# Attention probabilities and values as half precision pairs in a one-core trunk kernel

## The reference

```python
def _attend_block(qn, qr, qpos, kn, kr, v, kpos):
    s = jnp.einsum('bqhd,bkhd->bhqk', qn, kn) + jnp.einsum('bqhd,bkd->bhqk', qr, kr)
    s = s.astype(jnp.float32) * ATTN_SCALE
    allowed = (kpos // CHUNK)[None, :] <= (qpos // CHUNK)[:, None]
    s = jnp.where(allowed[None, None], s, -jnp.inf)
    p = jax.nn.softmax(s, axis=-1)
    return jnp.einsum('bhqk,bkhd->bqhd', p.astype(v.dtype), v)
```

## Time and profile before

| what | value |
|---|---|
| median of 3 runs | 1024.31 us (1024.24 to 1025.77) |
| the profiled execution's own time | 1023.69 us |
| its span in the profile | 1021.8 us |
| TensorE matmul busy | 980.3 us, 96% |
| TensorE weight loads busy | 759.5 us, 74% |
| VectorE busy | 814.5 us, 80% |
| ScalarE busy | 655.9 us, 64% |
| bytes moved | 205.01 MB, mean 201 GB/s |

### The profile page before, as it was taken

How to read it: one execution, slowest core, us unless ns; L and a number is a source line. 1 busy time by engine, 2 the same in 40 slices (tenths; PEclk the granted TensorE clock), 3 DMA queues, 4 the chain that set the end, 5 groups by cost and what they waited for, 6 DMA issues and landing times.

```text
span 1021.8 us, 24221 instructions
## 1 busy us (share of the span) xinstructions
PE 980.3 (96%) x9926; PEld 759.5 (74%) x9926; DVE 814.5 (80%) x1470; ACT 655.9 (64%) x1057; POOL 0.7 (0%) x10
## 2 busy tenths in 40 slices
PE   8999999999999999999999999999999989999995
PEld 6877777777776799976568777777777768998653
DVE  4897777654689899998888877776448899999986
ACT  5675454754355799876767645556543659987864
POOL 0000000000000000000000000000000000000000
PEclk9999999999999999999999999999999999999998
DMA  9845544423465199998736544452334435999961
GB/s 347 307 167 164 149 140 127 135 84 104 144 229 165 59 331 360 358 366 312 281 126 215 173 125 141 139 151 91 104 119 151 145 102 164 358 366 364 371 237 54
DMA packets 59651, 205.01 MB, mean 201 GB/s; under 512 B 7216, under 2 KB 10348, under 8 KB 59020
## 3 DMA queue, kind: packets, MB, share of 16 engines
q1 hardware_dynamic: 55980, 195.95, 55.2%
q10 hardware_dynamic: 3552, 7.42, 2.0%
HBM read 198.76 MB, written 3.40 MB: 198 GB/s over the span
## 4 chain that ended last, share of the span: by engine, by line
PE 64%; DVE 22%; DVEq 6%; ACT 4%; issue 3%; SPq 1%; DMA 1%; ACTq 0%
PE bank L1786 37%; DVE wlo L1075 12%; PE bank L1810 4%; DVEq L1709 4%; PE bank L2324 3%; ACT whi L556 2%; PE bank L2156 2%; PE bank L1815 1%; PE bank L2011 1%; DVE xT L1088 1%; DVE mo L1711 1%; DVE xlo L1094 1%; PE bank L2045 1%; DVE acc L1084 1%; PE bank L2087 1%
## 5 line engine op out<-in xcount | busy, mean ns | idle before, releaser
L1075 DVE SCALAR_TENSOR_TENSOR wlo<-w,whi 128x1024 f16<-128x1024 f32 x358 | 428.9, 1220 | 61.5 <-ACT whi L556 59.5
L556 ACT ACTIVATE whi<-w 128x1024 f16<-128x1024 f32 x358 | 369.0, 1049 | 81.4 <-PE bank L1786 48.1
L1786 PE MATMUL bank<-xhi,whi 128*128 128x320 f16 x688 | 206.2, 300 | 1.1 <-DVE wlo L1075 1.1
L1786 PE MATMUL bank<-xhi,wlo 128*128 128x320 f16 x688 | 205.7, 299 | 0.0
L1786 PE MATMUL bank<-xlo,whi 128*128 128x320 f16 x688 | 205.7, 299 | 0.0
L1786 PE MATMUL bank<-arena_b,whi 128*128 128x112 f16 x2048 | 161.7, 213 | 7.8 <-DVE wlo L1075 6.7
L1786 PEld LDWEIGHTS bank<-arena_b,whi 128*128 128x128 f16 x2048 | 149.5, 98 | 12.9 <-issue 9.0
L1786 PE MATMUL bank<-arena_b,wlo 128*128 128x112 f16 x1024 | 157.3, 213 | 0.0
L1786 PEld LDWEIGHTS bank<-arena_b,wlo 128*128 128x128 f16 x1024 | 100.1, 98 | 0.0
L1786 PEld LDWEIGHTS bank<-xhi,whi 128*128 128x128 f16 x688 | 67.2, 98 | 31.2 <-issue 3.0
L1786 PEld LDWEIGHTS bank<-xhi,wlo 128*128 128x128 f16 x688 | 67.3, 98 | 26.2
(11 more groups left out here) (379 smaller groups left out, 1761.1 us busy)
## 6 DMA issues: line engine op xcount, KB each, us to landing
w<-in_w SPq DMA_DIRECT2D x358, 512.0 KB, 5.1
arena_b<-head_rows ACTq DMA_DIRECT2D x2, 1920.0 KB, 7.1
xT<-in_x SPq DMA_DIRECT2D x2, 640.0 KB, 5.6
out_y<-xT SPq DMA_DIRECT2D x4, 320.0 KB
rows<-in_rows ACTq DMA_DIRECT2D x1, 1024.0 KB, 10.7
rows<-in_rows SPq DMA_DIRECT2D x1, 1024.0 KB, 6.4
out_ckv<-arena_a SPq DMA_DIRECT2D x2, 320.0 KB
acc<-kr SPq DMA_DIRECT2D x2, 288.0 KB
```

The source lines that it names most:

```text
L556: A(whi[:, n % SLOTS, :], w32[:, n % RAW, :], ACT.Copy, scale=WS).then_inc(hi_done.sem, 1)
L1075: V.scalar_tensor_tensor(wlo[:, n % SLOTS, :], w32[:, n % RAW, :], WS, whi[:, n % SLOTS, :], ALU.mult, ALU.subtract).then_inc(lo_done.sem, 1)
L1786: ins = M(out, w[:, s, sub * P:(sub + 1) * P], rhs(part, k), start=(n == 0), stop=(n == 3 * len(subs) - 1))
```

## The change

Probabilities and values are held as half precision pairs. A value item is copied by ScalarE in half precision (`v_out_hi`) and VectorE subtracts it for the rest (`v_out_lo`). The exponentials go to a single f32 buffer; VectorE multiplies the reciprocal by 4096; ScalarE writes the scaled probabilities in half precision (`probs_hi`) and VectorE the rest (`probs_lo`). The transposes are two matmuls each with a half precision identity, summed in PSUM; the result is split again by `columns_hi` and `columns_lo`. The values are three half precision products each. Turns are reordered: on TensorE the filler comes ahead of the values of u - 2 and the transposes of u - 1; on the other two engines the columns of u - 2 open the turn and the split of u closes it; rotation and query copies of half 1 move into turn 1, the rotation's sum into turn 2 ahead of the wait for the exponentials.

```diff
 # ScalarE
+                def probs_hi(u):
+                    act.wait_ge(p_inv.sem, p_inv.value(l, u + 1))
...
                 q_out(0)
                 hi_a(0)
                 k_out(0)
                 hi_a(1)
+                v_out_hi(0)
                 hi_a(2)
                 for u in range(UNITS):
+                    if u == 3:
+                        k_out(1)
+                    if u >= 2:
+                        columns_hi(u - 2)
                     if u in (5, 8, 11):
                         out_hi(u // 3 - 1)
-                    if u == 2:
-                        q_out(1)
-                    elif u == 3:
-                        k_out(1)
-                    elif u != 4:
+                    if u == 4:
+                        v_out_hi(1)
+                    elif u not in (2, 3):
                         gate_tanh(FILLER[u - 1] if u else 2)
-                    if u:
-                        probs_out(u - 1)
                     exps(u)
                     if u != 3:
                         hi_a(FILLER[u])
+                    if u == 1:
+                        q_out(1)
+                    probs_hi(u)
 # VectorE
                 for u in range(UNITS):
+                    if u >= 2:
+                        columns_lo(u - 2)
                     if u in (5, 8, 11):
                         out_lo(u // 3 - 1)
-                    if u == 2:
-                        rotate(1)
                     if u == 4:
-                        v_out(1)
+                        v_out_lo(1)
...
                     V.tensor_scalar(sm[:, 2:2 + w], sm[:, 0:w], -ATT_SCALE, None, ALU.mult
                                     ).then_inc(s_max.sem, 1)
+                    if u == 1:
+                        rotate(1)
+                    if u == 2:
+                        rotated(1)
                     dve.wait_ge(p_exp.sem, p_exp.value(l, u + 1))
                     V.reciprocal(sm[:, 6:6 + w], sm[:, 4:4 + w])
                     dve.drain()
...
+                    V.tensor_scalar(sm[:, 6:6 + w], sm[:, 6:6 + w], PS, None, ALU.mult
+                                    ).then_inc(p_inv.sem, 1)
-                    if u == 2:
-                        rotated(1)
                     if u != 3:
                         lo_a(FILLER[u])
+                    probs_lo(u)
 # TensorE
+                    def weigh(out, kt, rows_, vc, at, first, last):
+                        for x, y in ((0, 0), (0, 1), (1, 0)):
+                            a = M(out, v_hl[0:rows_, hf, x, kt, vc], prob_t[0:rows_, u % 2, y, at],
+                                  start=(first and x == 0 and y == 0), stop=(last and x == 1))
+                        return a
...
                 for u in range(UNITS):
                     scores(u)
-                    if u:
-                        transposes(u - 1)
-                    if u >= 2:
-                        values(u - 2)
...
                         gate(FILLER[u])
+                    if u >= 2:
+                        values(u - 2)
+                    if u:
+                        transposes(u - 1)
```

More of the change, by code:

```diff
@@ L64 @@
 GS = 1024.0
+PS = 4096.0
 BRANCHES = (1, 2, 0)
@@ L323, in build_trunk @@
         q_rot = sig("q_rot", 2)
+        v_hi = sig("v_hi", 6)
         v_ev = sig("v_ev", 6)
@@ L537, in _ @@
             nc.gpsimd.memset(gm16[:, :, :], 0.0).then_inc(consts_set.sem, 1)
-            for first in (num_ps, att_done, dc_ps, h_done, g_done, s_ps, sp_ps, o_lo, t_sb, stored, c_stored,
+            for first in (num_ps, att_done, dc_ps, h_done, g_done, s_ps, sp_ps, o_lo, t_lo, stored, c_stored,
                           m_used, yg_lo, e_free, e_prod, ot_ev):
@@ L782, in k_out, with v_out_hi @@
                         a.then_inc(qk_ev.sem, 1)
+                def v_out_hi(hf):
+                    if hf:
+                        act.wait_ge(stored.sem, stored.value(l, 16 * 4))
+                    for n in range(3):
+                        act.wait_ge(*item_done(l, hf, 8 + n))
+                        b = item_bank(ITEM0[hf] + 8 + n)
+                        if n < 2:
+                            a = A(v_hl[:, hf, 0, 2 * n:2 * n + 2, :], b[:, :].rearrange(
+                                "p (i n) -> p i n", i=2), ACT.Copy, scale=UN * XS)
+                        else:
+                            a = A(v_hl[0:TS, hf, 0, 4, :], b[0:TS, 0:2 * P], ACT.Copy, scale=UN * XS)
+                        a.then_inc(v_hi.sem, 1)
                 def gate_tanh(a):
@@ L2056, in transposes @@
                 def transposes(u):
-                    pe.wait_ge(p_norm.sem, p_norm.value(l, u + 1))
+                    pe.wait_ge(p_lo.sem, p_lo.value(l, u + 1))
                     if u:
-                        pe.wait_ge(t_sb.sem, t_sb.value(l, u))
+                        pe.wait_ge(t_lo.sem, t_lo.value(l, u))
                     for i in range(3):
                         n = P if u % 3 < 2 or i < 2 else TS
-                        a = TR(bank[6][0:n, i * P:(i + 1) * P], prob[:, u % 2, i * P:i * P + n],
-                               ident[:, :])
+                        for y in range(2):
+                            a = M(bank[6][0:n, i * P:(i + 1) * P], prob_h[:, u % 2, y, i * P:i * P + n],
+                                  mats16[:, 0, :], start=(y == 0), stop=(y == 1))
                     a.then_inc(t_ps.sem, 1)
@@ L2067, in values @@
                     hf, p, r = u // 6, u // 3 % 2, u % 3
-                    pe.wait_ge(t_sb.sem, t_sb.value(l, u + 1))
+                    pe.wait_ge(t_lo.sem, t_lo.value(l, u + 1))
                     if u % 6 == 0:
@@ L2109, in _ @@
                         gate(FILLER[u])
+                    if u >= 2:
+                        values(u - 2)
+                    if u:
+                        transposes(u - 1)
                 gate(14)
+                values(UNITS - 2)
                 transposes(UNITS - 1)
-                values(UNITS - 2)
                 gate(15)
```

119 lines of the change are left out of this document (73 added, 46 removed).

## The result

The changed kernel takes 1028.88 us (median of 6, 1028.5 to 1031.79) where the kernel before takes 1024.28 on the same chip: a ratio of 1.0048, interval 1.0035 to 1.0061, so slower by 0.35% to 0.61%. The forecast was 1029.0. The profiled execution took 1028.5 us with a span of 1026.4, that is 4.6 above the span before.

A forecast was written before the change was run, and what follows sets the result against it. TensorE's own work was taken to bound the attention stage. A layer: -1.2 + 2.9 + 0.1 + 0.6 = +2.4 us, two layers +4.8 on the median 1024.31, so about 1029 us; range 1022 to 1035.

The forecast's parts named there:

- TensorE's work: Attention stage: half precision values save 0.15 us eight times a layer, sample units and transposes nothing; -1.2 us a layer.
- cheap end of the bounds: Sample unit's values on TensorE: taken as unchanged, with +0.32 and -0.3 us as ends; the cheap one is -0.3.
- The wait in turn 3: TensorE waits about 2.9 us a layer before the values block, until ScalarE's late key copies free its bank; 2.0 to 3.8.
- Columns of unit 1: Behind turn 3's values block: they reach TensorE at 206.6 us, the block ends at 206.5, so 0.1 us more.
- The second wait: Turn 5: VectorE's share of unit 3 and the first output pair comes late, TensorE waits 0.6 us (0 to 1.2).
- No wait, faster: Rival: splits cheap or key copies free in time, only TensorE's smaller work is left; 1021 us, chance 0.15.
- VectorE as the bound: Rival: VectorE's cycle bounds the whole attention stage, with a surplus in every turn; 1035 us, chance 0.13.
- Half precision matmuls further apart: Rival: TensorE's small matmuls in transposes and values run about 0.08 us apart, not 0.056; 1038 us, chance 0.06.

The follow-up runs named there:

- Experiment 5: Changed kernel with key copies earlier, unit 1's columns split before unit 2's probabilities, half 1's value halves in turn 3: 1021.65 us against 1023.75 before, ratio 0.9976.
- (1): Changed kernel with ScalarE's eight key copies of half 1 moved from turn 3 into turn 2: 1023.75 us against 1023.72 before, ratio 1.0003.
- experiment 2: Changed kernel with the four rotation additions of turn 2 moved back behind VectorE's reciprocal and scaling: 1025.71 us, ratio 1.0022 to the kernel before.
- experiment 3: Changed kernel with the four rotation additions of half 1 run twice, writing the same values: 1033.32 us, ratio 1.0102 to the kernel before.
- experiment 4: Changed kernel with 17 unread matmuls of 320 columns on TensorE ahead of turn 3's values block: 1028.27 us, ratio 1.0048 to the kernel before.
- experiment 7: Changed kernel with TensorE's old order, transposes and values of earlier units ahead of the filler: 1037.84 us, ratio 1.0127 to the kernel before.
- experiment 8: Changed kernel with rotation and query copies back at the head of turn 2, additions at its end: 1027.08 us, ratio 1.0032 to the kernel before.
- experiment 6: Kernel before, still f32 in TensorE's old order, with only the moves of rotation, query copies and additions: 1023.21 us, ratio 0.9991.

## Why the prediction was right, point by point

**TensorE's work (predicted -1.2 us a layer).** Experiment 5 measures it all but without waits: 69.73 - 71.02 = -1.3. The total is right, its parts are not, and that it is right is in part luck. Three turns of the chain after, answering:

```profile
219.90 3.26 PE bank L1848 x24
223.16 0.62 PE bank L2141 x9
223.78 0.56 PE bank L2125 x6
224.34 0.85 PE bank L2107 x4
...
228.45 1.02 PE bank L2141 x18
229.48 0.44 PE bank L2125 x6
...
235.76 3.26 PE bank L1848 x24
```

235.76 - 219.90 = 15.86 us against 16.11: -0.25, where -0.30 was predicted. The prompt unit's values take 0.62 (predicted 0.65, before 0.80). The sample unit's take 1.02, not the unchanged 1.26: 18 matmuls of 64 columns came near the cheap end of the bounds. Here the prediction had miscounted: by its own prices the 12 records are 12 x 0.054 = 0.65 us and the 18 matmuls 18 x 0.027 = 0.49, so 0.16 less and not the same; and four changes of tile at 0.2 with the 0.65 make 1.45, more than the 1.26 they were read from. The transposes take 0.44 or 0.56, not 0.34, and scores behind them 0.71 or 0.85 against 0.66: going into and out of the 64-column tiles now shows there, where it showed in the filler (3.37) and the values before. The prediction left that out; before, too, the transposes behind a sample unit's scores took 0.48 in the chain and not 0.33. Summed over three turns by the two chains: values -0.60, fillers -0.22, transposes +0.30, scores +0.24, together -0.3 as forecast. The gain in the values is twice the forecast's, and what the forecast left out takes the other half back.

**The wait in turn 3 (predicted 2.9, bounds 2.0 to 3.8; measured 2.59 in both layers).** Each step can be held against the two timelines. Predicted and measured, by starts: VectorE's split of unit 0 at 191.52, 191.30; exponentials of unit 1 at 193.06, 192.86; query copies at 194.81, 194.61; ScalarE's half of unit 1 at 196.5, 196.28; VectorE's split of unit 1 at 197.35, 197.10; rotation additions at 199.27, 199.04; ScalarE's half of unit 2 at 201.75, 201.47; key copies at 202.2, 201.94; first bank free at 203.1, 202.80; wanted by TensorE at 200.2, and 202.80 - 2.59 = 200.21. VectorE's part and one row of ScalarE's, answering and the earlier trace rows:

```profile
191.30 0.35 DVE L1497 SCALAR_TENSOR_TENSOR mu_var<-mu_var,sm 128x128 f16<-128x128 f32 x1
...
191.96 0.28 DVE L1537 TENSOR_REDUCE sm<-bank 128x1 f32<-128x128 f32 x1
...
197.76 0.55 DVE L1510 TENSOR_TENSOR ysq<-bank,ysq 128x384 f16<-128x384 f32 x1
198.23 0.48 DVE L1540 TENSOR_REDUCE sm<-bank 128x1 f32<-128x320 f32 x1
...
196.28 0.39 ACT L830 ACTIVATE mu_var<-mu_var,sm 128x128 f16<-128x128 f32 x1
```

The split takes 191.96 - 191.30 = 0.66 between starts (0.65 was taken from a longer instruction of another stage), the columns 0.47 (0.50 taken), the hand-over of ScalarE's half of unit 1 to VectorE 0.82 (196.28 to 197.10; 0.85 put). No step of the two engines is off by more than some hundredths; they are 0.2 us sooner from the first one on, because the whole stage is (its first scores start at 186.23 after, 186.44 before). Counted from those scores, the bank is free after 16.57 us where the forecast has 203.1 - 186.44 = 16.66, and it is wanted after 13.98 where the forecast has 200.2 - 186.44 = 13.76. So of the 0.3 us of the miss 0.1 is the helpers' and 0.2 is TensorE's own way to the block, with the transposes and scores priced too low as above; that 200.2 was met to 0.01 is luck, the earlier start against the longer way. That this path makes the wait is shown by experiments as well: taking the copies off the path takes the wait away (1), taking the additions off the path shortens it by the 1.1 us of them that were not hidden (2), 2.0 us more on it are 2.0 us more of wait (3).

**Columns of unit 1 (predicted 0.1).** Layer 1: the block starts at 705.71 and, at the 3.50 us of before, ends at 709.21; the values behind it start at 709.36, right behind VectorE's columns in the chain: 0.15.

**The second wait (predicted 0.6, bounds 0 to 1.2).** It measured 0.5 in layer 1 and nothing in layer 0, where TensorE came to that place later than forecast, slowed by its clock. Experiments 2 and 4, without the fall, have it in layer 0 too.

**The clock (not predicted).** The text priced the wait by its length alone. In layer 0 the block behind it ran at half clock for three microseconds; the fall then swallowed the second wait, and experiment 4 puts its net price at 0.25 us. So layer 0 came to +2.5 and layer 1 to +2.2 where +2.4 was said of both; the sum is 4.7 against 4.8. In layer 1, without the fall, the parts as measured (-1.3, 2.6, 0.15, 0.5) make 2.0 of the 2.2; some of what is left is that pieces behind a wait are longer in the chain (a prompt unit's values 0.69 and 0.66 us behind the two, 0.62 else). So the closeness of the sum, 0.1 us, is more than the terms deserve: a wait 0.3 too dear stands against a clock and a restart that were not priced.

**The rivals.** *No wait, faster* fell: the key copies began at 201.94 and the first bank was free at 202.80, not before 201, and the splits took over 0.3 (0.35 and 0.48 for the two instructions of a prompt unit). Its price for the case, 2 x 1.2 = 2.4 us of gain, is what experiment 5 gives when its premise is made true (2.1 us of medians, 0.9976 with 0.9964 to 0.9988; 2.6 by the stages). *VectorE as the bound* fell: no wait on it after turn 5, three turns in 15.86 us, and in experiment 5 TensorE idle for 0.06. Its nearness was real, though, in turns 1 to 3: experiment 7 has the waits of turns 1 to 3 on exactly the column and probability halves that this rival named. *Half precision matmuls further apart* fell: nine in 0.62 us with a change of tile are at most 0.07 apart, and where nothing changes behind them six transposes take 0.34 from their first start to the next scores' (218.68 to 219.02 in the timeline), 0.06 each. The Trainium skill (TensorE: Matmul & The Clock Gate, Back-to-back issue gap) states about 81 ns a matmul for a real stream at this width. By that figure nine would take an estimated 0.73 us with nothing for the tile, and this trace's 0.62 disagrees with it.

## What to carry to other kernels

Where one engine bounds a stage, a change that lightens it and loads its helpers is worth what it takes from that engine only if each buffer still comes free in time; write out the helpers' program from one start, step by step, up to the copy that frees the first bank, and compare with the moment at which it is wanted. When such a wait appears, look first for work that stands ahead of the freeing copy without being needed by it: moving eight copies was worth 5 us here, more than the change itself (2.1 by the times, 2.6 by the stages). An instruction put ahead of a wait is hidden only until the other engine would have been through with its own work anyway; of the 1.98 us of rotation 0.9 were hidden, under the exponentials and ScalarE's weight block, and 1.1 were not.

## What was not expected of the hardware

After the same idle time TensorE's granted clock fell from 1.00 to 0.50 in one place and not in another. In the changed kernel it fell in layer 0 and not in layer 1 (2.59 us both times), in experiment 8 likewise (2.38 us both times, 0.20 us between starts in layer 0, 0.12 in layer 1, in the rows above); in experiment 7, behind waits of 2.38 us in turn 2, it fell in layer 1 and not in layer 0. After 4.6 us it fell in both layers (experiment 3), after 1.5 us in neither (experiment 2).

Nor does it go by the place in the code. In every trace TensorE waits 1.86 or 1.87 us once a layer, at the first matmul on `xhi` behind the layer norm that follows the output blocks: at 329.25 us in the kernel before and 329.27 in experiment 6, whose code is the same there. The windows behind these two (columns of the earlier trace rows), before and experiment 6:

```profile
330.00:333.00 3.00, 3.00 (x40) 2.27 (x39) 2.92 (x7) 1.69 (x3) 0.00 (x0) 1.00 0.11 42
```

```profile
330.00:333.00 3.00, 3.00 (x24) 1.83 (x23) 2.93 (x7) 1.68 (x3) 0.00 (x0) 0.54 0.14 55
```

Of the 20 such waits in the ten traces the clock fell behind three, one in experiment 6 and both in experiment 7; in experiment 6 the stretch between the two stages is 1.2 us longer for it (430.89 us against 429.67). So the same wait in the same code was followed by a lower clock in one execution and not in another, and a difference of a microsecond between two whole traces can be this alone. What decides it was not found; it stays open.

Where little covered it, the fall in experiment 8 cost 73.01 - 71.80 = 1.2 us (the same kernel and the same wait with it and without; the layer without it also had the second wait of 0.2), and where other data was late anyway, 0.25 (experiment 4).
